# A hybrid decoder step on one core: where x is turned, when exponentials, half of w_o and one expert's weights are due

## The reference

```
mod = silu(c) @ w_ada + b_ada                      # shift1, scale1, gate1, shift2, scale2, gate2
h = rmsnorm(x) * (1 + scale1) + shift1
q, k, v, b_gate, c_gate, u_in, gate_a, gate_b = split(h @ w_in)
o_attn = dilated attention, 3 groups of 4 heads, mixed by their denominators
o_conv = b_gate * conv3(c_gate * u_in)
merged = sigmoid(gate_a) * (o_attn @ w_pa) + sigmoid(gate_b) * (o_conv @ w_pb)
x = x + gate1 * (merged @ w_o)
h = rmsnorm(x) * (1 + scale2) + shift2
x = x + gate2 * moe(h)      # 4 groups of 8 experts: the best group, the best two experts in it
y = rmsnorm(x)
```

## Time and profile before

| | us |
|---|---|
| median of 3 runs (lowest, highest) | 834.04 (833.02, 834.59) |
| the profiled execution | 835.31 |
| its span, first to last instruction | 833.4 |
| TensorE busy with products | 708.1 (85%) |
| VectorE busy | 316.9 (38%) |
| ScalarE busy | 166.9 (20%) |
| mean granted TensorE clock | 0.930 of 2.4 GHz |
| moved by DMA | 198.98 MB |

### The profile page before, as it was taken

The page is one execution under the profiler, slowest core; times in us unless marked ns, Lnnn a source line. Parts: engine busy times, 40 slices in busy tenths (PEclk is TensorE's granted clock), DMA queues, the critical chain, the costliest instruction groups (busy, mean ns, idle before and its releaser), DMA issues.

```text
span 833.4 us, 12135 instructions
## 1 busy us (share of the span) xinstructions
PE 708.1 (85%) x5001; PEld 540.6 (65%) x5001; DVE 316.9 (38%) x691; ACT 166.9 (20%) x323; POOL 121.5 (15%) x186
## 2 busy tenths in 40 slices
PE   0799999999998699899997999779999978787810
PEld 0389898889998689799995455465565545454500
DVE  0362323136778443222323555425332221212145
ACT  0362222211342432022120111111111110101011
POOL 1500002110040000100000000122233222222011
PEclk9999999999999799999998999859999999999865
DMA  9834466873335027421106931487999999999863
GB/s 293 329 152 176 155 252 239 314 244 112 101 127 177 26 90 296 153 70 59 51 26 242 420 158 51 155 327 297 418 413 415 415 417 417 415 416 415 332 232 153
DMA packets 39199, 198.98 MB, mean 239 GB/s; under 512 B 7314, under 2 KB 7498, under 8 KB 23256
## 3 DMA queue, kind: packets, MB, share of 16 engines
q1 hardware_dynamic: 30272, 175.52, 53.8%
q0 software_dynamic: 8352, 21.81, 7.3%
q10 hardware_dynamic: 520, 0.87, 0.4%
HBM read 189.04 MB, written 17.40 MB: 248 GB/s over the span
## 4 chain that ended last, share of the span: by engine, by line
PE 77%; DVE 8%; DMA 5%; issue 4%; ACT 2%; SPq 2%; POOL 0%; POOLq 0%; DVEq 0%; ACTq 0%
PE bank L1531 29%; PE bank L1765 15%; PE bank L1784 7%; PE bank L1727 6%; PE bank L1675 4%; DMA arena_b<-in_w_ada 3%; PE bank L1754 2%; PE bank L1470 2%; PE bank L1672 2%; PE bank L1567 2%; PE bank L1692 1%; PE bank L1630 1%; DMA arena<-in_w_in 1%; PE bank L1720 1%; SPq L515 1%
## 5 line engine op out<-in xcount | busy, mean ns | idle before, releaser
L1531 PE MATMUL bank<-h_parts,w_parts 128*128 128x260 f32 x2160 | 275.8, 287 | 0.7 <-DVE w_parts L1011 0.5
L1531 PEld LDWEIGHTS bank<-h_parts,w_parts 128*128 128x128 f32 x2160 | 266.4, 191 | 9.8 <-issue 8.3
L1765 PE MATMUL bank<-arena,arena_b 128*64 128x256 f32 x704 | 88.6, 408 | 13.8 <-issue 12.8
L1765 PEld LDWEIGHTS bank<-arena,arena_b 128*64 128x64 f32 x704 | 56.6, 147 | 39.3 <-issue 16.2
L1011 DVE TENSOR_TENSOR w_parts<-arena,w_parts 128x1024 fp32r<-128x1024 f32 x46 | 56.3, 1224 | 66.4 <-ACT w_parts L857 66.2
L1360 DVE TENSOR_TENSOR arena_b<-bank,arena_b 128x128 f32<-128x128 f32 x32 | 9.3, 292 | 132.0 <-ACT arena_b L960 128.9
L1727 PE MATMUL bank<-arena,arena_b 128*128 128x512 f32 x128 | 58.6, 612 | 0.0
L800 POOL DMA_INDIRECT y_scratch<-arena_b x32 | 33.3, 1041 | 167.4 <-DVE arena_b L1381 157.3
L857 ACT ACTIVATE w_parts<-arena 128x1024 fp32r<-128x1024 f32 x46 | 48.4, 1053 | 42.6 <-DMA arena<-in_w_in 28.3
L1765 PE MATMUL bank<-arena_b 128*64 128x256 f32 x320 | 41.2, 415 | 11.0 <-issue 9.1
L1784 PE MATMUL bank<-arena,arena_b 128*64 128x512 f32 x196 | 47.0, 593 | 0.8 <-DVE arena_b L1366 0.8
(11 more groups left out here) (285 smaller groups left out, 760.7 us busy)
## 6 DMA issues: line engine op xcount, KB each, us to landing
arena<-in_w_gate_up SPq DMA_DIRECT2D x44, 1024.0 KB
arena<-in_w_in SPq DMA_DIRECT2D x46, 512.0 KB, 5.2
arena<-in_w_ada SPq DMA_DIRECT2D x22, 1024.0 KB, 7.1
arena<-in_w_down SPq DMA_DIRECT2D x22, 1024.0 KB
arena_b<-in_w_gate_up SPq DMA_DIRECT2D x20, 1024.0 KB
arena_b<-in_w_down SPq DMA_DIRECT2D x15, 512.0 KB
arena_b<-in_x_prompt SPq DMA_DIRECT2D x8, 512.0 KB, 13.8
arena<-in_w_o SPq DMA_DIRECT2D x2, 2048.0 KB, 8.2
```

The costliest lines, as they stand in the source:

```text
L1531: ins = pe.matmul(ps[s][:, 0:HALF], w_parts[:, n % 2, wp, k], h_parts[:, hp, k, s * HALF:(s + 1) * HALF], start=(k == 0 and hp == 1), stop ...
L1765: ins = pe.matmul(ps[2 + b][R * hh:R * hh + R, 0:2 * P], hTe[:, b, c * P + jj * R:c * P + jj * R + R], w_gu[slot][jj][:, c, :, hh * P:(hh ...
```

## The change

Front: x is loaded behind step 0 of w_ada, tile 0 of w_in behind step 3. TensorE turns the samples and three blocks of x between steps 1 and 2. Step 3 waits for its two loads one by one. The bias rows are loaded to 9 rows per quarter instead of 32, after SiLU, into a tile that VectorE clears. Attention: the exponentials go two sheets ahead; the samples' exponentials and their normalisation get places of their own in the list (`exp_s`, `norm_s`). Projection: the router's weights are loaded earlier, wo[1] in two parts, each when its place is free; the samples' halves are computed apart, with a prompt block's half between them, and `router(0)` and `ranks(0)` follow on both halves of the first prompt block; the router waits for each of its two copies. Experts: place 5 is loaded when the first gather has landed; the weighing stands behind the first expert's gate product. The semaphores of x's two loads are joined.

```diff
         plan.append(("spread",))
-        plan.append(("exp", 0))
-        plan.append(("samples", 0))
+        plan += [("exp", 0), ("exp", 1), ("samples", 0)]
         more_halves(1)
         for i in range(NS):
-            if i + 1 < NS:
-                plan.append(("exp", i + 1))
+            if i + 2 < NS:
+                plan.append(("exp", i + 2))
...
-            if i in (11, 12, 13):
-                plan.append((("turn_s",), ("pv_s",), ("join_s",))[i - 11])
+            if 9 <= i < 14:
+                plan.append((("exp_s",), ("norm_s",), ("turn_s",), ("pv_s",), ("join_s",))[i - 9])
...
                 for k in range(2):
-                    sp.dma_start(dst[:, k], ada_v[a // 4, a % 4, k]).then_inc(s_ada[min(a, 3)], 16)
+                    signal = s_ada_end if a == 3 and k == 1 else s_ada[min(a, 3)]
+                    sp.dma_start(dst[:, k], ada_v[a // 4, a % 4, k]).then_inc(signal, 16)
...
             for a in range(4):
-                if a == 3:
-                    load_tile(0)
                 load_ada(a)
-                if a == 1:
+                if a == 0:
                     for i in range(5):
                         sp.dma_start(x[0:rows[i], i], xp_v[i] if i < 4 else xs_v).then_inc(s_x[i], 16)
+            load_tile(0)
...
                     sp.dma_start(wo[0].rearrange("p k n -> p (k n)"), w_o[0]).then_inc(s_wo, 16)
-            sp.wait_ge(s_half, 2 * len(ORDER))
-            sp.dma_start(wrt.rearrange("p k n -> p (k n)"), w_router).then_inc(s_wr, 16)
-            sp.dma_start(rbias, b_router.to_broadcast([P, NG + NE])).then_inc(s_rb, 16)
-            sp.dma_start(wo[1].rearrange("p k n -> p (k n)"), w_o[1]).then_inc(s_wo, 16)
+                    sp.dma_start(wrt.rearrange("p k n -> p (k n)"), w_router).then_inc(s_wr, 16)
+                    sp.dma_start(rbias, b_router.to_broadcast([P, NG + NE])).then_inc(s_rb, 16)
+            for part in range(2):
+                sp.wait_ge(s_half, 2 * (len(ORDER) - 1 + part))
+                mine = slice(2 * D * part, 2 * D * (part + 1))
+                sp.dma_start(wo[1].rearrange("p k n -> p (k n)")[:, mine], w_o[1][:, mine]).then_inc(s_wo1[part], 16)
...
             sp.wait_ge(s_rt, 5)
+            sp.wait_ge(s_hg[0], 16)
             for half in range(2):
                 load_gate_up(5, 5, half)
                 load_down(5, 5, half)
...
+            act.wait_ge(s_c, 16 * 5)
+            act.activation(crow, crow, ACT.Silu).then_inc(s_csilu, 1)
+            act.wait_ge(s_bz, 1)
             for j in range(4):
-                src = b_ada[0].rearrange("(g j s n) -> j g (s n)", g=3, j=4, s=4)[j:j + 1]
-                act.dma_start(ada_bias[32 * j:32 * j + 32].rearrange("p (g s) n -> p g (s n)", g=3),
-                             src.to_broadcast([32, 3, 512])).then_inc(s_c, 16)
-            act.wait_ge(s_c, 16 * 9)
-            act.activation(crow, crow, ACT.Silu).then_inc(s_csilu, 1)
+                src = b_ada[0].rearrange("(g j n) -> j g n", g=3, j=4)[j:j + 1]
+                act.dma_start(ada_bias[32 * j:32 * j + 1 + TS].rearrange("p (g s) n -> p g (s n)", g=3),
+                              src.to_broadcast([1 + TS, 3, 512])).then_inc(s_bada, 16)
...
-            for a in range(3):
+            for a in range(2):
                 ada_step(a)
...
-            ada_step(3)
+            for a in range(2, 4):
+                ada_step(a)
             turn_x(3)
...
-                pe.wait_ge(s_h2c, 2 * n + 2)
                 for k in range(KD):
+                    if k % 4 == 0:
+                        pe.wait_ge(s_h2c, 2 * n + k // 4 + 1)
...
+            def project_samples(c):
+
+                for k in range(KD):
+                    if c and k % 4 == 0:
+                        pe.wait_ge(s_wo1[k // 4], 16)
+                    ins = pe.matmul(ps[2 + c][R * c:R * c + TS], mergedT[:, k, TP:T], wo[c][:, k], start=(k == 0),
+                                    stop=(k == KD - 1), skip_group_check=True)
+                ins.then_inc(s_wom[c], 1)
+
+            def project(n, c):
+                i = RB[n]
+                at_least(pe, s_x2, 2 * (n - 2) + c + 1 if n >= 2 else 0)
+                for k in range(KD):
+                    ins = pe.matmul(ps[2 + 2 * (n % 2) + c][:], mergedT[:, k, i * P:(i + 1) * P], wo[c][:, k],
+                                    start=(k == 0), stop=(k == KD - 1))
+                ins.then_inc(s_wom[c], 1)
+
+            project_samples(0)
+            project(1, 0)
+            project_samples(1)
+            project(1, 1)
+            router(0)
+            ranks(0)
+            for n in range(2, 5):
+                project(n, 0)
+                router(n - 1)
+                project(n, 1)
                 ranks(n - 1)
...
                 gate_up(e, e, e % SLOTS, 32 * (e // SLOTS + 1))
-                if e:
+                if e == 0:
+                    weigh()
+                else:
                     finish(e - 1)
```

More of the change, by code:

```diff
@@ L323, in hybrid_step @@
         s_c = sem("s_c")
+        s_bz = sem("s_bz")
         s_ada = [sem(f"s_ada{i}") for i in range(4)]
+        s_ada_end = sem("s_ada_end")
+        s_bada = sem("s_bada")
         s_win = [sem(f"s_win{i}") for i in range(WRING)]
@@ L329, in hybrid_step @@
         s_wo = sem("s_wo")
-        s_xr = [sem(f"s_xr{i}") for i in range(5)]
+        s_wo1 = [sem(f"s_wo1_{i}") for i in range(2)]
         s_eg = [sem(f"s_eg{i}") for i in range(SLOTS)]
@@ L394, in hybrid_step @@
         s_mrg = sem("s_mrg")
-        s_wom = sem("s_wom")
+        s_wom = [sem(f"s_wom{i}") for i in range(2)]
         s_x2 = sem("s_x2")
@@ L579, in _ @@
                 keep_x(n)
-            sp.wait_ge(s_wom, 10)
+            sp.wait_ge(s_wom[1], 5)
             for half in range(2):
@@ L929, in _ @@
                     ins.then_inc(s_exp, 1)
-                elif what == "qs" and a[0] == G - 1:
+                elif what == "exp_s":
                     act.wait_ge(s_qneg, 1)
@@ L987, in link @@
                 dve.wait_ge(s_dve, own[0])
+            dve.memset(ada_bias.rearrange("p c n -> p (c n)"), 0.0).then_inc(s_bz, 1)
             link(dve.memset(cvec.rearrange("p k r -> p (k r)"), 0.0))
@@ L1016, in ada_out @@
             def ada_out(g):
+                if g == 0:
+                    dve.wait_ge(s_bada, 64)
                 dve.wait_ge(s_adamm, 4 * g + 4)
@@ L1159, in _ @@
                                       ).then_inc(s_o, 1)
-                if what == "turn_s":
+                if what == "norm_s":
                     dve.wait_ge(s_qexp, 1)
@@ L1399, in _ @@
                 act_of(e, e)
-                if e:
+                if e == 0:
+                    dve.wait_ge(s_wsl, 1)
+                    link(dve.tensor_copy(per_slot[:, 2, 0:NE], ps[5][:, 0:NE]))
+                else:
                     down_of(e - 1, (e - 1) % EUN, 16 * ((e - 1) // EUN))
@@ L1468, in ada_step @@
                 for k in (first, first + 1):
+                    if a == 3 and k > first:
+                        pe.wait_ge(s_ada_end, 16)
                     for j in range(4):
@@ L1678, in _ @@
             pe.wait_ge(s_mrg, KD)
-            pe.wait_ge(s_wo, 32)
+            pe.wait_ge(s_wo, 16)
             def router(n):
@@ L1712, in _ @@
             pe.wait_ge(s_wr, 16)
-            for n, i in enumerate(RB):
-                r = rows[i]
-                at_least(pe, s_x2, 2 * (n - 1))
-                if n == 0:
-                    for k in range(KD):
-                        for c in range(2):
-                            ins = pe.matmul(ps[2 + c][R * c:R * c + r], mergedT[:, k, TP:T], wo[c][:, k],
-                                            start=(k == 0), stop=(k == KD - 1), skip_group_check=True)
-                            if k == KD - 1:
-                                ins.then_inc(s_wom, 1)
-                    continue
-                for c in range(2):
-                    for k in range(KD):
-                        ins = pe.matmul(ps[2 + 2 * (n % 2) + c][0:r], mergedT[:, k, i * P:i * P + r], wo[c][:, k],
-                                        start=(k == 0), stop=(k == KD - 1))
-                    ins.then_inc(s_wom, 1)
-                    if n and c == 0:
-                        router(n - 1)
+            def project_samples(c):
[22 more added lines that the diff above has]
+                project(n, 1)
                 ranks(n - 1)
@@ L1740, in _, with weigh @@
             pe.matmul(ps[7][:, 0:NE], ones, past[:, 5], start=True, stop=True, skip_group_check=True)
-            pe.wait_ge(s_ohw, 1)
-            for n, i in enumerate(RB):
-                r = rows[i]
-                for k in range(2):
-                    ins = pe.matmul(ps[5][:, 0:NE], oh_slot[0:r, i, k], oh_w[0:r, i, k], start=(n == 0 and k == 0),
-                                    stop=(n == 4 and k == 1), skip_group_check=True)
-            ins.then_inc(s_wsl, 1)
+            def weigh():
+                pe.wait_ge(s_ohw, 1)
+                for n, i in enumerate(RB):
```

(5 more changed lines are left out.)

12 lines of the change are left out of this document (5 added, 7 removed).

## The result

The changed kernel takes 825.62 us (median of 6 runs, 824.81 to 827.77), the kernel before in the same comparison 832.74 (831.64 to 834.59). The ratio is 0.9908, 95% interval 0.9894 to 0.9922: 7.7 us less by the ratio, 7.1 by the medians. I had forecast 829.2, 4.8 less than a median of 834.04. Of all executions in this document one is left out as slow: 1197.84 us, where the same kernel's five others (sample products side by side) took 814.4 to 815.9.

What follows compares the result with a forecast made beforehand. TensorE bounds the kernel almost throughout to 552 us, transfers set the pace after the first expert. -2.0 - 6.3 + 5.3 - 1.8 = -4.8 us against a median of 834.04: 829.2 us, range 824.5 to 833.4.

Steps and rivals of the forecast that it cites:

- output projection: Stretch from w_o's wait through sample products, routers and ranks: +5.3 us in sum, bounds -3.3 and +12.
- attention: Two TensorE waits around the samples' exponentials and normalisation become one of about 4 us: -6.3 us, 0.7 given back for clock.
- The front: Modulation at the start: last w_ada piece lands sooner, addition begins at 37.0 instead of 38.99, tile 0's split in its way: -2.0 us.
- Second half of w_o: Ahead of the output projection: loading this half in two parts, the first 6 us sooner, wins 2.2 us of TensorE's wait.
- seriality: In the output projection: sample products one after the other, a prompt product between, instead of side by side: 6.9 us more.
- the ranks' wait: Ahead of the first ranks, TensorE waits 2.45 us for VectorE's choice; the clock falling behind it costs +1.7.
- Experts: First experts: first gather takes 2.7 us instead of 6.18 with place 5 held back; weighing delays turned activations 1.6: -1.8 us.
- rival C: Output projection: sample products filling 8 of 128 columns don't lift the clock; in full 841.1 us, slower; chance 0.08.
- A: Output projection: sample products cost nothing extra in a row (0.22 per instruction), 6.9 off the sum: 822.3 us; chance 0.12.
- B: Attention: the wait only changes its name, samples turned 3 us sooner, not 7; +3 to +4, 832.8 us; chance 0.12.
- D: Front gains 4.5 us, the split not in the way, and the first experts' gathers 3.4: 825.1 us; chance 0.10.
- three marks for being wrong: Samples turned later than 285, four projections in under 25 us, or the front's addition starting before 36.

Runs made afterwards that it cites:

- the attention run: The changed kernel with only the attention plan of before put back (exponentials one sheet ahead, samples' exponentials and normalisation at their old places): 832.6 us, ratio 0.9996.

## Why the prediction fell short

**What failed** is a term of the output projection: "each later router starts its products behind the first of two copies (1.08 us for both): 3 x 0.5 sooner, and 0.7 in the last". The waits are of that size (0.74 and 0.25), but I priced the wait alone. I had asked of every wait that the change adds whether the clock falls behind it, and gave back 1.7 for the ranks; I didn't ask it of the waits that it removes. In the profile before, the last projection took 8.81 us where the others took 7.11 to 7.13, and I never asked why:

```profile
522.97 1.98 PE L1692 MATMUL bank<-arena_b,arena 128*128 128x36 f32 x16 [0.74 <-ACT arena L830]
524.78 8.81 PE L1727 MATMUL bank<-arena,arena_b 128*128 128x512 f32 x16
```

Measured alone, the edit is worth 3.6 us in the kernel before and some 5 in the changed one, not 2.2.

**What was mis-sized** is attention: 7.6 us in the traces, not 6.3 (6 to 7 in the times, which don't exclude 6.3). Of the surplus 0.7 is the clock that I gave back for one longer wait: it costs nothing, since the stretch behind the turn is 161.14 us with the new plan and 161.12 with the old. The rest is in the walk itself, where the samples were turned 7.0 sooner by the forecast and 7.6 in the trace: the sheet ahead of the split is the two exponentials of 0.79.

**The front** came out near its 2.0 (1 to 2 us by its run), but partly by luck. The addition that I read at 38.99 stood behind a step of 2.79 us, partly at half clock; with the same front it is 1.92 us and the addition comes at 37.9 to 38.1 in three other profiles, here the kernel before with the router edit:

```profile
35.87 1.92 PE L1470 MATMUL bank<-arena_b 128*32 128x512 f32 x16 [1.77 <-DMA arena_b<-in_w_ada]
...
37.86 0.69 DVE L1018 TENSOR_TENSOR arena_b<-bank,arena_b 128x512 f32<-128x512 f32 x1 [4.65 <-PE bank L1470]
```

So the addition moves by some 1.2 us, and 0.9 of the 2.0 was a low clock of the profile before. The mechanism held: the split is in the way. By the Trainium skill (DMA: Bandwidth & Descriptors, Why a DMA increments its semaphore by 16 and not by 1) the bias copies would have spared less and the last piece would have landed 0.5 us later than by the mean rate, an estimate. The traces lie between: the piece lands at 33.1 to 33.4 us in seven profiles with the new front and at 35.9 to 36.15 in four with the old, 2.75 apart on the mean, where the mean rate gave 3.0 and that page 2.5. No row shows single engines.

**What held.** Second half of w_o: the wait of 4.54 us became 2.33 (2.2 forecast). Projections: +8.3 against +8.0, with seriality 7.0, the ranks' wait 2.64 and the clock 1.5 behind it. Experts: -2.5 for the last router and the gathers together, as forecast; but only the sum fits. The router's part there is 0.4 (37.94 us in the kernel before with that edit, 38.32 without; forecast 0.7), and holding place 5 back is worth 4.6 in the trace and 2.5 to 3.2 in the times (forecast 3.4, less 1.6 for the weighing). With the measured prices the sum is -1.5 - 7.6 - 2.2 + 8.3 + 1.5 - 3.2 - 2.5 = -7.2 us, near the 7.1 between the medians. The terms are from traces except the first, which is the middle of its run's 1.1 to 1.9; several are uncertain by 1 us, so the closeness is luck. One bound of the prediction was added wrongly: rival C adds 11.9 to the +5.3 of the output projection, so the upper bound was +17, not +12.

**The base.** The profiled executions differ by 10.0, not by 7.1. The first profile of the kernel before stood 2.6 us above its own median of six, the changed kernel's 0.4 below its own, and the low clock of 1.5 us at 220, which comes and goes, is in the first and not in the second. I had set the base only 1.3 above a median of three.

**The rivals.** A (sample products free in a row) falls: 7.03 us for 16. B falls with the attention run. C falls: the clock rose after 3.2 us of these products. D's front falls. Its gathers (3.4) are not shown: the first gate product comes 3.7 us sooner behind the last projection, but at least 1 of that is the last router's, since with its wait put back the first gather is issued 1.06 us later behind the projection. Of my three marks for being wrong none was met: samples turned at 277.9, four projections in 29.7 us, the addition at 36.66. They were drawn around places and not around the sum, so none watched the stretch that failed.

Not tried: what the ranks' wait and its clock cost apart from each other, at what length between 0.25 and 0.74 us the routers' waits begin to cost a low clock, and why the clock at the start of the sample products was low in most profiles but not in two.

## What to carry to other kernels

Read every instruction group of the kernel before for members that are slower than their like (8.81 beside 7.11), and ask what stands ahead of them: a short wait that repeats can cost more through the clock behind it than by its length. Products that use few columns are worth pairing in different columns of the array; in a row each costs a full one. When one profile is the base of a sum, first ask how far it stands from the median of more runs.

## What the runs showed of the hardware

- Three waits of 0.74 us, some 18 us apart in otherwise full work, brought the clock from 2.4 to 1.2 GHz once in each of three profiles, behind the third in the two of the kernel before and behind the second in the kernel with that wait put back. Three of 0.25 us did in none of eleven.
- Two groups of products that write different columns of the array overlap even where one stands wholly behind the other in the order: four of them ran beside the last of the first group, some 1.7 us won without any interleaving (13.88 us for 32 products). With a 128-column product between them there is none of it (16 products in 7.03 us).
- The same order of TensorE's work from the first tiles on, with the same wait of 1.34 us at 216 to 219 us, was followed by a low clock of some 1.5 us in 6 profiles of 14 and by none in 8.
